# Second block: norms by tokens, with a turned tile scaled by two engines

## The reference, cut to what matters

```python
        x = rms_norm(x, g_final[l])                      # end of the first block
...
    for l in range(DEPTH_2):                             # second block, two layers
        mod = c @ w_ada[l] + b_ada[l]
        shift, scale, gate = jnp.split(mod, 3, axis=-1)
        h = _layer_norm(x, LN_EPS) * (1.0 + scale[:, None, :]) + shift[:, None, :]
        proj = h @ w_in[l]
...
        y = jnp.concatenate([y_attn, y_conv, y_four], axis=-1) @ w_out[l]
        x = _layer_norm(DEEPNORM_ALPHA * x + (1.0 + gate[:, None, :]) * y, LN_EPS) * ln_g[l] + ln_b[l]
```

## Time and profile before

| | us |
|---|---|
| median of 3 runs | 3617.12 (3616.16 to 3622.07) |
| the profiled execution's own time | 3616.27 |
| its span, first to last instruction | 3614.4 |
| PE busy in the span | 3367.9 (93%) |
| VectorE busy | 2106.4 (58%) |
| ScalarE busy | 1270.0 (35%) |

### The profile page before, as it was taken

The page is one execution under the profiler, slowest core; times in us unless marked ns, Lnnn a source line. Parts: engine busy times, 40 slices in busy tenths (PEclk is TensorE's granted clock), DMA queues, the critical chain, the costliest instruction groups (busy, mean ns, idle before and its releaser), DMA issues.

```text
span 3614.4 us, 39331 instructions
## 1 busy us (share of the span) xinstructions
PE 3367.9 (93%) x16050; PEld 2709.7 (75%) x16050; DVE 2106.4 (58%) x2505; ACT 1270.0 (35%) x1779; POOL 410.9 (11%) x503
## 2 busy tenths in 40 slices
PE   6999999999997699999999999899799989998997
PEld 4788888887785578878888887468678846876885
DVE  7555555555745689475555554651389566126974
ACT  3222222232231178342222223331178243215852
POOL 0000000021101122110101002010012001000210
PEclk8999999999997699999999999999999999998999
DMA  4222222225442458212222222142351203325221
GB/s 189 93 82 82 94 80 83 93 60 111 172 144 99 82 74 87 71 59 84 103 82 84 80 93 71 37 123 78 105 60 41 77 12 106 117 79 88 43 64 47
DMA packets 141266, 309.76 MB, mean 86 GB/s; under 512 B 55096, under 2 KB 80476, under 8 KB 130080
## 3 DMA queue, kind: packets, MB, share of 16 engines
q1 hardware_dynamic: 80928, 215.51, 19.0%
q0 software_dynamic: 60160, 91.74, 12.0%
HBM read 255.04 MB, written 52.18 MB: 85 GB/s over the span
## 4 chain that ended last, share of the span: by engine, by line
PE 85%; DVE 8%; ACT 3%; DMA 2%; issue 1%; POOL 0%; SPq 0%; ACTq 0%; DVEq 0%
PE psum L727 39%; PE psum L817 12%; PE psum L786 10%; PE psum L1096 5%; PE psum L1110 5%; PE psum L1086 4%; PE psum L828 3%; PE psum L1207 1%; PE psum L925 1%; PE psum L1197 1%; ACT attn_num L1649 1%; PE psum L919 1%; DVE w_lo L1815 1%; DMA fo_alt<-in_alternating 1%; DVE ln_xc L2394 1%
## 5 line engine op out<-in xcount | busy, mean ns | idle before, releaser
L1815 DVE TENSOR_TENSOR w_lo<-w_raw,w_hi 128x1024 fp32r<-128x1024 f32 (+1 forms) x135 | 227.4, 1684 | 354.3 <-ACT w_hi L1322 354.3
L1322 ACT ACTIVATE w_hi<-w_raw 128x1024 fp32r<-128x1024 f32 (+1 forms) x135 | 191.5, 1419 | 260.7 <-PE psum L727 130.2
L727 PE MATMUL psum<-a_hi,w_hi 128*128 128x512 f32 x704 | 276.7, 393 | 5.5 <-DVE a_lo L1937 3.8
L727 PE MATMUL psum<-a_hi,w_lo 128*128 128x512 f32 x704 | 275.1, 391 | 0.0
L727 PE MATMUL psum<-a_lo,w_hi 128*128 128x512 f32 x704 | 275.0, 391 | 0.0
L2301 DVE TENSOR_TENSOR attn_tl<-psum,attn_th 128x512 fp32r<-128x512 f32 x384 | 247.1, 684 | 23.1 <-ACT attn_th L1640 19.4
L1096 PEld LDWEIGHTS psum<-mats,attn_num 128*128 128x128 f32 x1536 | 168.9, 143 | 109.1 <-ACT attn_num L1649 108.0
L1640 ACT ACTIVATE attn_th<-psum 128x512 fp32r<-128x512 f32 x384 | 209.4, 596 | 114.4 <-PE psum L1096 106.8
L1096 PE MATMUL psum<-mats,attn_num 128*128 128x128 f32 x1536 | 214.6, 284 | 31.9 <-ACT attn_num L1649 31.1
L2005 DVE SCALAR_TENSOR_TENSOR x<-psum,cols,x 128x1024 f32<-128x1024 f32 x144 | 184.3, 1282 | 93.6 <-PE psum L727 93.4
L2295 DVE TENSOR_REDUCE attn_sm<-psum 128x1 f32<-128x1024 f32 x128 | 156.2, 1221 | 31.5 <-PE psum L1086 31.5
(11 more groups left out here) (520 smaller groups left out, 8501.2 us busy)
## 6 DMA issues: line engine op xcount, KB each, us to landing
w_raw<-in_w_ada SPq DMA_DIRECT2D x52, 1024.0 KB, 4.9
w_raw<-in_w_gu SPq DMA_DIRECT2D x44, 1024.0 KB, 4.9
w_raw<-in_w_in SPq DMA_DIRECT2D x34, 1024.0 KB, 4.9
w_raw<-in_w_down SPq DMA_DIRECT2D x22, 1024.0 KB, 4.9
w_raw<-in_w_out SPq DMA_DIRECT2D x12, 1024.0 KB, 6.5
qk_hi_scratch<-p_out_hi POOLq DMA_DIRECT2D x18, 512.0 KB, 3.0
qk_lo_scratch<-p_out_lo POOLq DMA_DIRECT2D x18, 512.0 KB, 3.8
w_early<-in_w_ada SPq DMA_DIRECT2D x8, 1024.0 KB, 18.2
```

Of the source, the lines that this page charges most:

```text
L727: mm = e.matmul(bank, a[:, k * width + m * P:k * width + (m + 1) * P], b(k, h), start=(ends[0] and k == order[0] and i == 0), stop=(ends[1 ...
L1322: e.activation(like(src, hi), src, ACT.Identity).then_inc(*w_hi.mark(n, part))
L1815: e.tensor_tensor(like(src, lo), src, like(src, hi.bitcast(F32)), ALU.subtract).then_inc(*w_done.mark(n, part))
```

## The change

The residual of the second block is kept by tokens: `t.x[:, j, :]` is 128 tokens (on the partitions) by 1024 features, for j = 0 to 7. A sum over features is then a sum along a row of a tile, and comes out of an instruction as one column (`accum_out`); means and roots are columns of 128x1 in `norm_cols`.

- *Stretch A.* PE turns each token tile of x (eight transposes of 128x128 into a pair of banks, `turn_tokens`, "x"); ScalarE squares it with a row sum, VectorE multiplies by g_final with a row sum into `o[j]`, the columns of both norms are worked out (`inverse_root`, `second_norm`), ScalarE makes the normed tile z, PE turns it back ("z"), and h is made from the turned tile: VectorE scales and shifts the first four slices of 128x128, ScalarE the other four, which lie in the other bank (`H_DVE = (4, 4)`). ScalarE rounds h in two copies, VectorE subtracts in two. VectorE's rounds 0 to 3 stand behind the updates of x by feature tiles 2, 3, 4 and 6 of the second half, rounds 4 to 9 behind that of tile 7, so the update by tile 7 stands behind round 3. The table `TURNS_1` sets the order on PE: the first six turns stand between the feature tiles of ffn2's second half, the others and the four half passes ("p", output tile, token half) of the input projection's first two tiles after it.
- *Stretches B and C.* `out_proj_tokens` makes a bank of 128 tokens by 512 features at a time (j, c), 24 matmuls each, again 384 in all: six token tiles of the left half (c = 0) come first, with the last heads' part added when it is there. VectorE multiplies the bank by 1 + gate and adds it to the residual with a row sum (`gained`), then norms the row. In layer 0 layer 1's opening norm follows in the same round of VectorE and ScalarE (`out_tokens`, `tokens_2`), and PE's turns of z stand between banks of the output projection.
- The old `stat_x`, `layer_norm`, `stat_total`, `gemm_pair`, the statistics after ffn2 and four fences go. x times ALPHA moves from VectorE before the output projection to ScalarE (layer 0: after stretch A, eight instructions; layer 1: one in each block of the input projection). Blocks 2 and 3 of the output weights get tiles of their own and are rounded before it. GpSimd loads three rows (gate, ln_g, ln_b), spread over the partitions. The result leaves as eight stores of 128x1024.

The diff, cut to its core (tile placement, signals, GpSimd and SyncE left out, eight columns of indentation taken off):

```diff
+TURNS_1 = (("x", 0), ("x", 1), ("x", 2), ("z", 0), ("x", 3), ("z", 1), ("z", 2), ("x", 4), ("x", 5), ("z", 3), ("x", 6),
+   ("p", 0, 0), ("z", 4), ("x", 7), ("z", 5), ("p", 1, 0), ("z", 6), ("z", 7), ("p", 0, 1), ("p", 1, 1))
+TURNS_2 = (("p", 0, 0), ("z", 5), ("p", 1, 0), ("z", 6), ("z", 7), ("p", 0, 1), ("p", 1, 1))
...
+def turn_tokens(l, what, j):
+    if what == "x":
+        p = ps.take(e, ("tokens", j), ln_cols, "minus", 0, j, 1)
+        e.wait_ge(*x_new.at("ffn2", "half", KT - 1, j // 4))
+        for k in range(KT):
+            mm = e.transpose(p.full[:, k * P:(k + 1) * P], t.x[:, k, j * P:(j + 1) * P], ident)
+        mm.then_inc(*x_turned.mark(j))
+    else:
+        p = ps.take(e, ("normed", l, j), ln_hi, l, j)
+        e.wait_ge(*ln_z.at(l, j))
+        for k in range(KT):
+            mm = e.transpose(p.full[:, k * P:(k + 1) * P], t.b2[l].z[j % 2][:, k * P:(k + 1) * P], ident)
+        mm.then_inc(*z_turned.mark(l, j))
...
+                if n == 2 and h == 1 and 1 <= dd < KT - 1:
+                    turn_tokens(0, *next(turns))
...
+def out_proj_tokens(l):
+    m, name, at_name = t.b2[l], f"mix2{l}", f"attn2_{l}"
+    banks = {}
+    def part(j, c, ks, ends):
+        if ends[0]:
+            banks[j, c] = ps.take_bank(e, ("out", name, j, c), ln_x, "gained", l, j, c)
+        for k in ks:
+            if j == 0 and c == 0:
+                e.wait_ge(*mix_lo.at(name, "ab"[k // 4], k % 4))
+            src = m.mixb if k // 4 else m.mixa
+            (whi, wlo), o = places[2 * c + k // 4][1:], (k % 4) * HALF
+            for i, (a, w) in enumerate(((0, whi), (0, wlo), (1, whi))):
+                mm = e.matmul(banks[j, c], src[a][:, k % 4, j * P:(j + 1) * P], w[:, o:o + HALF],
+                              start=(ends[0] and k == ks[0] and i == 0), stop=(ends[1] and k == ks[-1] and i == 2))
+        if ends[1]:
+            mm.then_inc(*tile_done.mark("out", name, j, c))
+            if j == ST - 1:
+                for place in places[2 * c:2 * c + 2]:
+                    tile_done.value[("block", place[0], 0)] = tile_done.count
+    places = [block(("out2", l, i)) for i in range(2)]
+    rows = last_sums_place(at_name)
+    for j in range(BEFORE):
+        part(j, 0, (0, 1, 2), (True, False))
+        if j == 1:
+            last_sums(at_name, rows)
+    for j in range(BEFORE):
+        part(j, 0, (4, 5, 6, 7), (False, False))
+    every = (0, 1, 2, 4, 5, 6, 7, 3)
+    for j in range(BEFORE):
+        part(j, 0, (3,), (False, True))
+        if j == 0:
+            continue
+        if j == 1:
+            places += [block(("out2", l, i)) for i in (2, 3)]
+        part(j - 1, 1, every, (True, True))
+        if l == 0 and j >= 4:
+            turn_tokens(1, "z", j - 4)
+    part(BEFORE - 1, 1, every, (True, True))
+    for turn, (j, c) in enumerate(((6, 0), (7, 0), (6, 1), (7, 1))):
+        part(j, c, every, (True, True))
+        if l == 0 and turn >= 1:
+            turn_tokens(1, "z", turn + 1)
...
+    for what, *which in (TURNS_1[6:], TURNS_2)[l]:
+        if what != "p":
+            turn_tokens(l, what, *which)
+            continue
+        m_, h = which
+        if h == 0:
+            ps.take(e, firsts[m_], rope_act, "raw", firsts[m_])
+            ps.keep(firsts[m_])
...
+def squares_of(l, j, which, src, scale, bias, over, epsc):
+    e.activation(t.sq[:], src, ACT.Square, scale=scale, bias=bias,
+                 accum_out=ln_col(j, which, SQ)).then_inc(*ln_squares.mark("sum", l, j, which))
+    e.wait_ge(*ln_squares.now())
+    e.activation(ln_col(j, which, GUESS), ln_col(j, which, SQ), ACT.Abs_reciprocal_sqrt, scale=1.0 / over,
+                 bias=epsc).then_inc(*ln_squares.mark(l, j, which))
...
+def normed(l, j):
+    m = t.b2[l]
+    e.wait_ge(*ln_cols.at("normed", l, j))
+    if j >= 2:
+        e.wait_ge(*z_turned.at(l, j - 2))
+    e.activation(m.z[j % 2][:], m.o[j][:] if l == 0 else t.x[:, j, :], ACT.Identity,
+                 scale=ln_col(j, 1, PROD if l == 0 else HALF_R), bias=ln_col(j, 1, VAR)).then_inc(*ln_z.mark(l, j))
+def to_h(l, j):
+    m, p = t.b2[l], ps.of[("normed", l, j)].full
+    e.wait_ge(*z_turned.at(l, j))
+    if j:
+        e.wait_ge(*ln_lo.at(l, j - 1))
+    elif l == 0:
+        e.wait_ge(*ln_dve.at("scales"))
+    for k in range(H_DVE[l], KT):
+        c = slice(k * P, (k + 1) * P)
+        e.activation(m.hf[:, c], p[:, c], ACT.Identity, scale=scale_col(l, k), bias=shift_col(l, k)).then_inc(
+            *ln_h.mark(l, j))
+    if H_DVE[l]:
+        e.wait_ge(*ln_dve.at("h", l, j))
+    e.wait_ge(*ln_h.now())
+    for part, dst in enumerate((m.ha, m.hb)):
+        src = m.hf[:, part * HALF:(part + 1) * HALF].rearrange("p (k q) -> p k q", k=4)
+        e.activation(dst[0][:, :, j * P:(j + 1) * P], src, ACT.Identity).then_inc(*ln_hi.mark(l, j))
...
+def tokens_1():
+    for j in range(ST + 2):
+        if j < ST:
+            first_squares(-1, j)
+        if 1 <= j <= ST:
+            normed(0, j - 1)
+        if j < ST:
+            second_squares(0, j)
+        if j >= 2:
+            to_h(0, j - 2)
+        if j == 0:
+            blocks.get(("down", 2, LAST_GROUP, 1))
+    e.wait_ge(*ln_cols.at("residual"))
+    for j in range(ST):
+        e.activation(t.x[:, j, :], t.b2[0].o[j][:], ACT.Identity, scale=ln_col(j, 0, PROD)).then_inc(*x_tok.mark(0, j))
+    e.wait_ge(*x_tok.now())
...
+def tokens_2():
+    for j in range(ST + 2):
+        if j == ST:
+            normed(1, j - 1)
+        if j >= 2:
+            to_h(1, j - 2)
+        if j < ST:
+            if j == 6:
+                blocks.get(("out2", 0, 3))
+            first_squares(0, j)
+            if j:
+                normed(1, j - 1)
+            second_squares(1, j)
...
+def inverse_root(l, j, which, over, eps):
+    c = [ln_col(j, which, i) for i in range(9)]
+    e.wait_ge(*ln_squares.at(l, j, which))
+    e.tensor_scalar(c[VAR], c[SQ], 1.0 / over, eps, ALU.mult, ALU.add).then_inc(*ln_cols.mark("var", l, j, which))
+    e.wait_ge(*ln_cols.now())
+    small(c[VAR], c[GUESS], c[VAR], c[GUESS], ALU.mult, ALU.mult, "times var", l, j, which)
+    small(c[HALF_R], c[VAR], -3.0, c[GUESS], ALU.add, ALU.mult, "root", l, j, which)
...
+def to_h(l, j):
+    m, p = t.b2[l], ps.of[("normed", l, j)].full
+    e.wait_ge(*z_turned.at(l, j))
+    if j:
+        e.wait_ge(*ln_lo.at(l, j - 1))
+        e.wait_ge(*ln_hi.at(l, j - 1))
+    for k in range(H_DVE[l]):
+        c = slice(k * P, (k + 1) * P)
+        e.tensor_scalar(m.hf[:, c], p[:, c], scale_col(l, k), shift_col(l, k), ALU.mult, ALU.add).then_inc(
+            *ln_dve.mark("h", l, j))
...
+    for j in range(ST + 2):
+        if j < ST:
+            e.wait_ge(*ln_squares.at("sum", 0, j, 0))
+            e.tensor_tensor_reduce(out=o[j][:], in0=ps.of[("tokens", j)].full, in1=t.acc[:], scale=1.0, scalar=0.0,
+                                   op0=ALU.mult, op1=ALU.add, accum_out=ln_col(j, 0, SUM)).then_inc(*ln_x.mark("o", j))
+        if 1 <= j <= ST:
+            second_norm(0, j - 1)
+        if j < ST:
+            inverse_root(0, j, 0, D, EPS)
+            e.wait_ge(*ln_x.at("o", j))
+            small(ln_col(j, 1, MINUS), ln_col(j, 0, SUM), -1.0 / D, ln_col(j, 0, HALF_R), ALU.mult, ALU.mult,
+                  "minus", 0, j, 1)
+        if j >= 2:
+            to_h(0, j - 2)
+            low_tokens(0, j - 2)
+        if j == ST - 1:
+            e.tensor_scalar(t.ln[:, :, 0, PROD:PROD + 1], t.ln[:, :, 0, HALF_R:HALF_R + 1], -0.5 * ALPHA, None,
+                            ALU.mult).then_inc(*ln_cols.mark("residual"))
+        yield
...
+def gained(l, place, j, c):
+    m, half = t.b2[l], slice(c * HALF, (c + 1) * HALF)
+    n = place.next()
+    by = t.acc[:, (n % 2) * HALF:(n % 2 + 1) * HALF]
+    e.wait_ge(*tile_done.at("out", f"mix2{l}", j, c))
+    if n >= 2:
+        e.wait_ge(*ln_x.at("place", l, n - 2))
+    e.tensor_tensor(by, ps.of[("out", f"mix2{l}", j, c)], m.gain[:, half], ALU.mult).then_inc(
+        *ln_x.mark("gained", l, j, c))
+    e.wait_ge(*ln_x.now())
+    e.wait_ge(*x_tok.at(l, j))
+    e.tensor_tensor_reduce(out=t.x[:, j, half], in0=t.x[:, j, half], in1=by, scale=1.0, scalar=0.0,
+                           op0=ALU.add, op1=ALU.add, accum_out=ln_col(j, 0, SUM + c)).then_inc(*ln_x.mark("x", l, j, c))
+    ln_x.value[("place", l, n)] = ln_x.count
+def out_tokens(l):
+    m, place, ahead = t.b2[l], Counter(), {0: 4, 1: 5, 4: 6, 5: 7}
+    e.wait_ge(*row_in.at("rows", l))
+    for j in range(BEFORE - 2):
+        gained(l, place, j, 0)
+    for j in range(ST + 2 if l == 0 else ST):
+        if j < ST:
+            gained(l, place, j, 1)
+            e.wait_ge(*ln_x.now())
+            e.tensor_scalar(ln_col(j, 0, MINUS), ln_col(j, 0, SUM), ln_col(j, 0, SUM_B), -1.0 / D, ALU.add,
+                            ALU.mult).then_inc(*ln_cols.mark("minus", l, j, 0))
+        if l == 0 and 1 <= j <= ST:
+            second_norm(1, j - 1)
+        if j < ST:
+            e.wait_ge(*ln_cols.at("minus", l, j, 0))
+            if j:
```

(18 more changed lines are left out.)

400 lines of the change are left out of this document (194 added, 206 removed).

## The result

| | before | changed |
|---|---|---|
| median of 4 runs | 3616.64 (3614.22 to 3622.07) | 3590.09 (3584.84 to 3592.21) |
| ratio | | 0.9922, 95% interval 0.9905 to 0.9940 |
| the profiled execution and its span | 3616.27, 3614.4 | 3584.84, 3583.0 |

The change takes 26.6 us off. The forecast was added up for the profiled execution, as 3586.5, and 3584.84 came; this execution is the shortest of its four (the others took 3588.5 to 3592.2), so part of that agreement is chance. The sum also hides larger errors of its terms.

The account below looks back on a forecast made before the run. It took PE, with 85% of the chain, as the bound apart from waits for norms. 3616.3 + 10.5 - 12.9 - 27.4 gave 3586.5, so a median of 3587; eight in ten from 3561 to 3607.

Parts of the forecast that it names:

- Stretch A: From ffn2's last group, second half, to the end of the input projection's first pass: 99.3 before, 109.8 forecast, 10.5 more.
- Prices of the steps: Costs of single steps from near trace rows: four 128x128 slices 1.5 on ScalarE, 1.2 on VectorE; one-column steps 0.20 to 0.26.
- Hand-offs: Release of a dependent step on another engine or the same one: priced at 0.03 to 0.1, PE's at 0.14.
- The rival with 0.13 more: All 26 rounds: 0.13 more on every release would cancel the gain, giving 3617; chance of slower 0.08.
- The ring of 9.1: Middle round in A: ScalarE and VectorE wait for each other, so 128 tokens take 9.1, despite 7.2 and 5.7 of work.
- The update by tile 7: In A, x's update by feature tile 7 stands behind round 3 and ends at 44.4, where before it ended at 24.
- Stretch B: From layer 0's output projection to the end of layer 1's first pass: 172.5 before, 159.5 forecast, saving 13.
- Stretch C: From layer 1's output projection to the span's end: 128.2 before, 100.8 forecast, saving 27.4, called the surest part.
- the sign that was named: Profile after, layer 1's end: final tiles of x 5.6 and 7.0 apart, end about 12 after PE's last matmul.
- Better overlap: Rounds in A and B: lower step prices give 3574, A's rounds at ScalarE's own 7.2 give 3565; chance 0.2.
- The cold clock: PE's pieces between waits stay at 1.2 GHz: A +3, B +8, total 3598; chance 0.1.
- the rival of dear hand-offs: All 26 rounds: each 0.1 more per release adds 23 us, 0.2 more gives 3637; chance of slower 0.08.

Follow-up runs that it names:

- split_0_0: The changed kernel with all eight slices of each turned tile scaled on ScalarE, none on VectorE: 3600.64 us, 0.9960 of before.
- extra_step: The changed kernel with one more dependent one-column VectorE step in each inverse root, 40 steps in all: 3591.75 us, 0.9928 of before.
- round3_behind: The changed kernel with VectorE's round 3 in stretch A behind the update of x by feature tile 7: 3586.62 us, 0.9920 of before.
- warm: The changed kernel with matmuls that nobody reads filling four PE waits, two in A and two in B: 3589.00 us, 0.9915 of before.
- warm_pair: The changed kernel with 26 unread matmuls, into a free pair of banks, before layer 0's last output projection bank: 3587.84 us, 0.9923 of before.

## Why the prediction was right, point by point

- **What bounds.** The three stretches carry 29.8 of the 31.4 between the spans. Right.
- **Prices of the steps.** Four slices took 1.37 on VectorE (1.2 was taken) and 1.48 on ScalarE (1.5). The line through 512 and 1024 columns gave 0.28 for a slice on VectorE. They start 0.32 apart there, and 0.34 apart on ScalarE. From the cycles that the Trainium skill, VectorE: DVE Perf Modes, section The TRN2 errata, gives for a source in PSUM, an estimate is 0.26 on VectorE and 0.25 on ScalarE. The measurement decides: 0.32 and 0.34. Its advice against small tiles fits the trace: four slices took 1.37, one step of 512 columns 0.69. split_0_0 shows that ScalarE's slices lie on the path one for one.
- **Hand-offs.** 0.03 to 0.1 was right: a one-column step of VectorE with its release is 0.20 (extra_step), and from ScalarE to VectorE the last fence below has under 0.05 (the guess ends at 3558.83 + 0.29 = 3559.12, VectorE goes on at 3559.16). The rival with 0.13 more is refuted where the rounds hold such steps.
- **Stretch A.** 108.2 for 109.8. Products of tiles 0 to 7 ended at 11.2, 17.7, 23.7, 33.9, 46.7, 55.5, 64.4, 77.4; forecast were 10.3, 17, 23, 34, 47.6, 56.7, 65.8, 78.6. The ring of 9.1 is 8.82. The half pass in front of round 7 was priced at 3.7, and moving it gave 3.3. The update by tile 7 (44.4, measured 42.2) was described rightly and costs nothing by itself (round3_behind).
- **Stretch B: the step that failed.** 164.3 for 159.5. Up to round 6 the rounds were right to within 1.2 (the first steps of the right halves ended at 46.2, 54.3, 62.0, 71.9, 81.9, 98.6, 109.8; forecast 46.1, 54.6, 62.5, 72.8, 83.1, 98.3, 110.0). Then two terms were missing. I added a slow start "to each first half pass after a wait", but not to a bank of the output projection: after 8.79 it cost 8.3 - 5.4 = 2.9. And I let z 5 turn at once, though the half pass (0, 0) stands before it and waits 6.96 for the weight block that I had myself put into round 6. Tile 7's right half came at 127.6 for 125.2, so 2.4 late. Tile 5's h ended at 137.0 after B's start, tile 7's at 151.3 where 146.8 was forecast: 4.5 of the 4.8. Edits of these two waits gave 4.1 and 1.4 alone and 7.3 together (6.4, 3.7 and 9.6 against the B of the same group).
- **Stretch C.** 98.0 for 100.8. A round is 5.35 and 6.69, where 5.6 and 7.0 stood: the last step occupies VectorE for 1.21 and not 1.4 (the next begins before its sum is read), the mean 0.25 for 0.3, the root 0.83 for 0.9. The seven gaps between the output tiles add up to 42.8 where 45.2 was forecast: 2.4 of the 2.8. So the sign that was named, the end some 12 after PE's last matmul, missed: that matmul ends at 3574.0 and the span at 3583.0, 9.0 later. The rounds themselves, right half, mean, square and guess, root, last step, are those of the forecast (VectorE's rows and, between them, ScalarE's guess):

```profile
3555.84 0.69 DVE L2593 TENSOR_TENSOR ada_acc<-psum,lno_row 128x512 f32<-128x512 f32 x1
...
3557.30 0.21 DVE L2611 TENSOR_SCALAR norm_cols<-norm_cols 128x1 f32<-128x1 f32 x1
3557.55 1.28 DVE L2619 SCALAR_TENSOR_TENSOR ln_v<-x,norm_cols,lno_row 128x1024 f32<-128x1024 f32 x1
3558.83 0.29 ACT L1760 ACTIVATE norm_cols<-norm_cols,eps 128x1 f32<-128x1 f32 x1
3559.16 0.15 DVE L2519 TENSOR_SCALAR norm_cols<-norm_cols 128x1 f32<-128x1 f32 x1 [0.32 <-ACT norm_cols L1760]
...
3559.98 1.28 DVE L2632 SCALAR_TENSOR_TENSOR x<-ln_v,norm_cols,lno_row 128x1024 f32<-128x1024 f32 x1
...
3561.19 0.69 DVE L2593 TENSOR_TENSOR ada_acc<-psum,lno_row 128x512 f32<-128x512 f32 x1
```

- **Rivals.** Better overlap: its floor of 7.2 for a round in A wasn't reached, since the order of waits in the code holds. The cold clock: it came at restarts in A and B, at up to 2.9 a time. That rival had 8 for B. It was a part of the truth, which I had given a chance of 0.1 as a whole.
- **The total** was right to 3 us by luck in the terms: A 1.6 and C 2.8 too high, B 4.8 too low.
- **Slips in the sums**, none of which moves the forecast by more than 1: the steps of a round in C add up to 5.7, not 5.6, and the rival of dear hand-offs adds up to 24 for each 0.1 and to 3635 at 0.2, not to 23 and 3637.

## What to carry to other kernels

When work is cut into rounds that pass between engines, write the ring down (what each waits for, in the order of the code) and put every instruction of it on it, the weight rounding too: in A and C the sum of a round told its length to 5%, the busy shares told nothing. For each wait of TensorE allow for its restart, wherever it is (here it cost from nothing to 2.9), and look at what stands behind the waiting instruction in its queue. Before reading a difference of 1 or 2 in such a stretch as the work of an edit, look whether the restarts ahead of the edited place are alike in the two profiles. Of slices that either engine could do, give them to the one that waits in the ring, and measure the split in each stretch: four and four was worth 13.0 in stretch A against all on ScalarE, and eight to VectorE there gave 2.3 more.

## What the runs showed of the hardware

- Matmuls that nobody reads, run in a wait, keep the granted clock at 1.00 for the real ones: 5.6 instead of 7.8 for the half pass (0, 0) of A (warm), 5.6 instead of 8.3 for a bank of B (warm_pair). With 1.2 to 2.0 of the wait left behind them (five places) none of the real ones was slow; 14 that stopped 4.1 early left 13 slow ones. They have to write to banks that are free: 32 into a pair that VectorE still had to read waited 9.29 with the rest.
- The number of slow matmuls at the same place differs between executions, 2 to 4 in five profiles and 7 to 10 in six at one bank of B, and shifts what comes behind by 1.6.
- 128x128 slices out of PSUM with scale and bias as columns start 0.32 apart on VectorE and 0.34 on ScalarE; a one-column step with its release takes 0.20 on VectorE.
